# A depthwise convolution on TensorE: taps as pairs of 64x64 quarters, and gating between the granules of the projection

## The reference

```python
proj = u @ conv_w_in                                   # 256 x 1024 by 1024 x 1792
glu_in, mq = jnp.split(proj, [2 * CONV_DIM], axis=-1)  # CONV_DIM = 768
a, gate = jnp.split(glu_in + b_in, 2, axis=-1)
u = a * jax.nn.sigmoid(gate)
# causal, per channel, 31 taps: u[t] = sum_i dw[i] * u[t - 30 + i] + dw_b
u = depthwise_conv(u, dw) + dw_b
mix = jax.nn.silu(layer_norm(u, ln_g, ln_b))           # over the 768 channels
mem_out = memory_attention(mq, mk, mv, g_mq, g_mk)     # 4 heads of 64, 256 memory tokens
h = h + jnp.concatenate([mix, mem_out], axis=-1) @ w_out
```

## Time and profile before

| | us |
|---|---|
| three runs | 1823.68, 1824.05, 1825.80 |
| their median | 1824.05 |
| the profiled execution | 1827.86 |
| its span | 1826.1 |
| mean granted TensorE clock of its span | 0.984 of full |

### The profile page before, as it was taken

How to read it: one execution, slowest core, us unless ns; L and a number is a source line. 1 busy time by engine, 2 the same in 40 slices (tenths; PEclk the granted TensorE clock), 3 DMA queues, 4 the chain that set the end, 5 groups by cost and what they waited for, 6 DMA issues and landing times.

```text
span 1826.1 us, 22665 instructions
## 1 busy us (share of the span) xinstructions
PE 1756.5 (96%) x8300; PEld 1448.8 (79%) x8300; DVE 1346.3 (74%) x1211; ACT 1161.0 (64%) x1149; POOL 63.1 (3%) x64
## 2 busy tenths in 40 slices
PE   7899999989999998879999999999999999999998
PEld 6678888877788886668888888888888888888886
DVE  5664444675554457658888888888898888888888
ACT  5555553665444447547777777677777777776775
POOL 1110000230000010020000000000000000000000
PEclk9899999999999999889999999999999999999999
DMA  9554553644655561038989999999999999999995
GB/s 339 165 165 159 183 186 121 194 152 153 195 183 185 162 206 50 23 105 307 369 327 365 371 325 367 350 349 365 346 348 372 328 370 367 323 370 347 348 368 224
DMA packets 226406, 480.82 MB, mean 263 GB/s; under 512 B 11796, under 2 KB 48296, under 8 KB 226352
## 3 DMA queue, kind: packets, MB, share of 16 engines
q1 hardware_dynamic: 217056, 470.99, 72.6%
q10 hardware_dynamic: 9296, 9.11, 1.5%
HBM read 478.99 MB, written 2.65 MB: 264 GB/s over the span
## 4 chain that ended last, share of the span: by engine, by line
PE 53%; DVE 4%; ACT 3%; issue 2%; ACTq 0%; DVEq 0%; POOLq 0%; POOL 0%
PE bank L614 16%; PE bank L617 16%; PE bank L615 16%; PE bank L1125 2%; ACT w_hi L1661 1%; PE bank L1157 1%; PE bank L1038 1%; DVE x L2175 1%; DVE w_lo L2195 1%; ACT L1661 0%; DVE dwy L2076 0%; DVE stat L2076 0%; ACT y_hi L1649 0%; DVE w_lo L1718 0%; DVE rawmax L1815 0%
## 5 line engine op out<-in xcount | busy, mean ns | idle before, releaser
L2195 DVE TENSOR_TENSOR w_lo<-raw,w_hi 128x2048 fp32r<-128x2048 f32 x336 | 764.4, 2289 | 118.5 <-ACT w_hi L1661 115.5
L1661 ACT ACTIVATE w_hi<-raw 128x2048 fp32r<-128x2048 f32 x336 | 639.2, 1919 | 173.5 <-PE bank L617 173.4
L1718 DVE TENSOR_TENSOR w_lo<-raw,w_hi 128x2048 fp32r<-128x2048 f32 (+3 forms) x118 | 257.1, 2184 | 158.7 <-ACT w_hi L1227 158.4
L614 PE MATMUL bank<-w_hi,xg_hi 128*128 128x512 f32 x896 | 355.5, 397 | 5.8 <-DVE w_lo L2195 4.3
L617 PE MATMUL bank<-w_hi,xg_lo 128*128 128x512 f32 x896 | 350.4, 391 | 0.0
L615 PE MATMUL bank<-w_lo,xg_hi 128*128 128x512 f32 x896 | 349.9, 390 | 0.0
L1227 ACT ACTIVATE w_hi<-raw 128x2048 fp32r<-128x2048 f32 (+3 forms) x118 | 213.1, 1811 | 104.0 <-PE bank L617 93.2
L614 PE MATMUL bank<-w_hi,a_hi 128*128 128x512 f32 (+3 forms) x672 | 261.8, 390 | 14.1 <-DVE a_lo L2110 5.4
L615 PE MATMUL bank<-w_lo,a_hi 128*128 128x512 f32 (+3 forms) x672 | 255.5, 380 | 0.0
L617 PE MATMUL bank<-w_hi,a_lo 128*128 128x512 f32 (+3 forms) x672 | 255.3, 380 | 0.0
L614 PEld LDWEIGHTS bank<-w_hi,xg_hi 128*128 128x128 f32 x896 | 168.9, 189 | 42.4 <-DVE w_lo L2195 7.3
(11 more groups left out here) (226 smaller groups left out, 1695.4 us busy)
## 6 DMA issues: line engine op xcount, KB each, us to landing
raw<-in_moe_w_gate SPq DMA_DIRECT2D x114, 1024.0 KB, 6.8
raw<-in_moe_w_up SPq DMA_DIRECT2D x113, 1024.0 KB, 7.0
raw<-in_moe_w_down SPq DMA_DIRECT2D x112, 1024.0 KB, 6.3
raw<-in_w_mlp SPq DMA_DIRECT2D x32, 1024.0 KB, 5.2
raw<-in_ffn_w_gate SPq DMA_DIRECT2D x22, 512.0 KB, 3.8
raw<-in_ffn_w_up SPq DMA_DIRECT2D x22, 512.0 KB, 4.8
raw<-in_ffn_w_down SPq DMA_DIRECT2D x11, 1024.0 KB, 4.9
raw<-in_w_in SPq DMA_DIRECT2D x10, 1024.0 KB, 12.2
```

The costliest lines, as they stand in the source:

```text
L614: pe.matmul(o, hi, h, start=start, stop=False)
L1661: act.activation(w_hi[:, g % NSPLIT, :], raw_at(g, GRAN), ACT.Copy).then_inc(hi_made, 1)
L1718: dve.tensor_tensor(w_lo[:, g % NSPLIT, 0:n], raw_at(g, n), w_hi[:, g % NSPLIT, 0:n].bitcast(F32), ALU.subtract).then_inc(lo_made, 1)
L2195: dve.tensor_tensor(w_lo[:, g % NSPLIT, :], raw_at(g, GRAN), w_hi[:, g % NSPLIT, :].bitcast(F32), ALU.subtract).then_inc(lo_made, 1)
```

## The change

- **The projection.** The jobs become: value and gate columns of channel tiles 0 and 1 (512 columns, 256 of each, by two DMAs a granule), `mq` (256 columns), value and gate of tiles 2 and 3, value and gate of tiles 4 and 5. So a pair of tiles can be transposed and gated (`glu_t`, `gates`, `gated`) as soon as its own job is done. Transposes, scores, softmax and values of the memory attention are put between the granules, as in the other two blocks.
- **The taps.** TensorE takes 20 of the 31 taps, two at a time. A tap pair is four float32 matmuls of 64 rows by 64 columns, one for each quarter of the array: tap 2i on channels 0-63 (rows 0-63, columns 0-63) and on channels 64-127 (rows and columns 64-127), and tap 2i+1 on the two other quarters, which read `glu_x`, a copy of `glu` with its two halves of partitions exchanged. `glu_x` is made by DMAs inside SBUF (`crossed`, two of 64 x 2 x 256 for each pair of tiles), issued by ScalarE. The upper and the lower 64 rows write different banks, and VectorE adds both banks (`add_taps`). ScalarE writes two diagonals of 128 x 64 for a pair (`dw` and `dw_x`, a copy of the weights with exchanged halves), in a ring of 12 pairs. Each quarter counts its own semaphore `tap_used[n]`.
- **VectorE** takes 11 taps a tile, two tiles by turns, so that the second sum in `stat` falls away.
- **`out2`** begins with the memory attention's tiles: these are multiplied before the mean is known and while the squares are made. The rounded halves of the normalized tiles are made one tile at a time.

The core of the diff; the parts left out are the same edits on names, and the helpers `gates`, `gated`, `out_in2`, which wrap the loops of before:

```diff
-PE_TAPS = 16
-N_DIAG = 12
+PE_TAPS = 20
+TAP_PAIRS = PE_TAPS // 2
+DIAG_PAIRS = 12
+TAP_BANK = (2, 4, 0, 2, 0, 4)
...
-    stage("glu", t="adadad")
-    stage("qk2", t="aa")
-    stage("pv2", t="bb")
+    stage("mk2", t="a")
+    stage("glu0", t="ad")
+    stage("mq2", t="a")
+    stage("glu1", t="ad")
+    stage("pvm2a", t="b")
+    stage("pvm2b", t="b")
+    stage("glu2", t="ad")
...
-    CONV_JOBS = [(0, 512), (512, 512), (1024, 512), (1536, 256)]
+    CONV_JOBS = [(0, 512), (1536, 256), (512, 512), (1024, 512)]
...
+        if n == 256:
+            project(conv_in, c0, n)
+            continue
+        for half in range(2):
+            stream.append(([(rows(conv_in, half * 512, 4, u * CONV_TILES * P + c0 // 2, 256), None, u) for u in range(2)], 4, 512))
...
+        glu_x = sb("glu_x", [P, CONV_TILES, S + DW_K - 1], stack=layer)
...
-        diag = dwq[:].rearrange("p k s -> p (k s)").rearrange("p (n c) -> p n c", c=P)
-        stat = sb("stat", [P, 3, S], stack=layer)
+        diag = dwq[:].rearrange("p k s -> p (k s)").rearrange("p (n c) -> p n c", c=HD)
...
+            def mq2_t(kk):
+                if kk == 2:
+                    copied(j2 + 1)
+                    cols_t(at["mq2"]["t"], proj2, [MQ2, MQ2 + P])
+            def taps(k):
+                pe.wait_ge(glu_x_in[k // 2], 32)
+                ba, bb = bank[TAP_BANK[k]], bank[TAP_BANK[k] + 1]
+                for i in range(TAP_PAIRS):
+                    m = k * TAP_PAIRS + i
+                    pe.wait_ge(diag_made, 2 * m + 2)
+                    for n, (w, u, r, c, b) in enumerate(((0, glu, 0, 0, ba), (0, glu, HD, HD, bb),
+                                                         (1, glu_x, 0, HD, ba), (1, glu_x, HD, 0, bb))):
+                        tap = 2 * i + w
+                        mm = pe.matmul(b[c:c + HD, 0:S], diag[r:r + HD, 2 * (m % DIAG_PAIRS) + w, :], u[r:r + HD, k, tap:tap + S],
+                                       start=i == 0, stop=i == TAP_PAIRS - 1)
+                        mm.then_inc(tap_used[n], 1)
...
+            in2(0)
+            in2(1)
             pe.wait_ge(qk_made, 5)
-            t = at["qk2"]["t"]
-            cols_t(t, proj2, [MQ2, MQ2 + P])
-            cols_t(t + 1, kvm2, [0, P])
-            pe.wait_ge(t_act, act_steps(t + 1))
-            def taps(k):
-                if k >= 2:
-                    pe.wait_ge(dw_acc, k - 1)
-                for i in range(PE_TAPS):
-                    pe.wait_ge(diag_made, k * PE_TAPS + i + 1)
-                    mm = pe.matmul(bank[k % 2][:, 0:S], diag[:, (k * PE_TAPS + i) % N_DIAG, :], glu[:, k, i:i + S],
-                                   start=i == 0, stop=i == PE_TAPS - 1)
-                    mm.then_inc(tap_used, 1)
-                means = {4: (0, 1, 2), 5: (3,)}.get(k, ())
-                if k == 4:
-                    pe.wait_ge(s_exp, 4 * len(PAIRS))
-                for done in means:
-                    channel_mean(done)
-            def channel_mean(k):
-                return pe.matmul(bank[2][:, 0:S], onesm[:], dwy[:, k, :], start=k == 0, stop=k == CONV_TILES - 1)
-            pe.wait_ge(t_dve, dve_steps(at["glu"]["t"] + 5))
+            cols_t(at["mk2"]["t"], kvm2, [0, P])
+            in2(2)
+            glu_t(0)
+            in2(3)
+            in2(4, mq2_t)
+            pe.wait_ge(t_act, act_steps(at["mq2"]["t"]))
             scores(MEM2)
-            taps(0)
+            in2(5)
             scores(MEM2 + 1)
             probs_t(MEM2)
-            taps(1)
+            in2(6, lambda kk: glu_t(1) if kk == 2 else None)
             values(MEM2)
             probs_t(MEM2 + 1)
+            in2(7)
+            values(MEM2 + 1)
+            glu_t(2)
+            pe.wait_ge(s_exp, 4 * len(PAIRS))
+            taps(0)
+            pe.wait_ge(p_sb, 2 * len(PAIRS))
+            taps(1)
             taps(2)
-            values(MEM2 + 1)
-            for k in range(3, CONV_TILES):
-                taps(k)
-            pe.wait_ge(dw_acc, CONV_TILES)
+            pe.wait_ge(dw_acc, 1)
+            taps(3)
+            pe.wait_ge(t_dve, dve_steps(at["glu2"]["t"] + 1))
+            pe.wait_ge(t_dve, dve_steps(at["pvm2b"]["t"]))
+            channel_mean(0)
+            channel_mean(1)
+            channel_mean(2)
+            taps(4)
+            channel_mean(3)
+            taps(5)
...
+            out2_part(0, 0, (0,))
             for k in range(4, CONV_TILES):
                 mm = channel_mean(k)
             mm.then_inc(mu_psum, 1)
+            out2_part(0, 0, (1,))
+            out2_part(1, 0, (0, 1))
             for k in range(CONV_TILES):
                 pe.wait_ge(sqc_made, k + 1)
-                mm = pe.matmul(bank[3][:, 0:S], onesm[:], dwq[:, k, :], start=k == 0, stop=k == CONV_TILES - 1)
+                mm = pe.matmul(bank[7][:, 0:S], onesm[:], dwq[:, k, :], start=k == 0, stop=k == CONV_TILES - 1)
             mm.then_inc(var_psum, 1)
-            def fill_out2(i, kk):
-                if i == 0 and kk % 2 == 0:
-                    pe.wait_ge(ln_lo, kk // 2 + 1)
-                if i == 0 and kk == 0:
-                    pe.wait_ge(dw_acc, CONV_TILES)
-                    pe.wait_ge(cent_made, CONV_TILES)
-                    pe.wait_ge(sd_made, 1)
-                if i == 2 and kk == 0:
-                    pe.wait_ge(ln_lo, 3)
-                if i == 2 and kk == 2:
-                    pe.wait_ge(t_dve, dve_steps(PAIRS[MEM2 + 1].t))
-            out_jobs("out2", "mix2", "nffn1", fill_out2)
+            out2_part(0, 0, (2, 3))
+            out2_part(1, 0, (2, 3))
+            out2_part(0, 1, range(4))
+            out2_part(1, 1, range(4))
...
+            def crossed(p):
+                act.wait_ge(t_dve, dve_steps(at[f"glu{p}"]["t"] + 1))
+                for r in (0, HD):
+                    act.dma_start(glu_x[r:r + HD, 2 * p:2 * p + 2, DW_K - 1:], glu[HD - r:P - r, 2 * p:2 * p + 2, DW_K - 1:])\
+                        .then_inc(glu_x_in[p], 16)
+            def diagonals(first, last):
+                for m in range(first, last):
+                    k, i = divmod(m, TAP_PAIRS)
+                    if m >= DIAG_PAIRS and (m % 2 == 0 or m == first):
+                        for n in range(4):
+                            act.wait_ge(tap_used[n], m - m % 2 - DIAG_PAIRS + 2)
...
+                    for w, taps in enumerate((dw, dw_x)):
+                        act.activation(diag[:, 2 * (m % DIAG_PAIRS) + w, :], ident2[:], ACT.Copy,
+                                       scale=taps[:, k, 2 * i + w:2 * i + w + 1]).then_inc(diag_made, 1)
+            act.wait_ge(kv_act, 2)
+            act.wait_ge(kv_dve, 2)
+            square_heads(kvm2, 0, MEM_HEADS, None)
+            for r in (0, HD):
+                ins = act.activation(ident2[r:r + HD, :], ident[r:r + HD, r:r + HD], ACT.Copy)
+            chained(ins)
+            hi_to(g + 3)
...
+            gates(0)
+            hi_to(g + 5)
+            crossed(0)
+            out_in2(1)
+            square_heads(proj2, MQ2, MEM_HEADS, j + 1)
+            hi_to(g + 6)
+            t_copy(at["mq2"]["t"], memq[:], GMQ1)
             exps(MEM2)
-            diagonals(1)
+            hi_to(g + 7)
+            out_in2(2)
             probs_copy(MEM2)
             exps(MEM2 + 1)
+            hi_to(g + 8)
+            gates(1)
             mixed_hi(MEM2)
-            diagonals(2)
             probs_copy(MEM2 + 1)
-            diagonals(3)
+            crossed(1)
+            hi_to(g + 9)
+            diagonals(0, 6)
+            out_in2(3)
             mixed_hi(MEM2 + 1)
-            diagonals(4)
-            hi_to(at["out2"]["g"] + 2)
-            diagonals(CONV_TILES - 1)
+            gates(2)
+            diagonals(6, 12)
+            crossed(2)
+            diagonals(12, 20)
+            hi_to(g + 10)
+            diagonals(20, CONV_TILES * TAP_PAIRS)
...
+                act.wait_ge(silu2, k + 1)
+                act.activation(a_at(a_hi, "mix2", 2 + k)[:, 0, :], dwq[:, k, :], ACT.Copy).then_inc(ln_hi, 1)
...
+            def other_taps(p, first, last):
+                for i in range(PE_TAPS + first, PE_TAPS + last):
+                    for k in (2 * p, 2 * p + 1):
+                        u, y = glu[:, k, i:i + S], dwy[:, k, :]
+                        if i == PE_TAPS:
+                            ins = dve.tensor_scalar(y, u, dw[:, k, i:i + 1], dwb[:, k:k + 1], ALU.mult, ALU.add)
+                        else:
+                            dve.wait_ge(dve_own, own[0] - 1)
+                            ins = dve.scalar_tensor_tensor(y, u, dw[:, k, i:i + 1], y, ALU.mult, ALU.add)
+                        own[0] += 1
+                        ins.then_inc(dve_own, 1)
...
+                y = dwy[:, k, :]
+                chained(dve.tensor_tensor(y, y, bank[TAP_BANK[k]][:, 0:S], ALU.add))
+                dve.tensor_tensor(y, y, bank[TAP_BANK[k] + 1][:, 0:S], ALU.add).then_inc(dw_acc, 1)
...
+            sum_heads(N2MK)
+            chained(dve.memset(glu[:, :, 0:DW_K - 1], 0.0))
```

(87 more changed lines are left out.)

136 lines of the change are left out of this document (44 added, 92 removed).

## The result

The changed kernel takes 1807.76 us (median of five runs, 1806.51 to 1813.17). The kernel before takes 1825.80 us in five runs beside it. The ratio is 0.9901, 95% interval [0.9888, 0.9914]: 18 us, 1%, faster. The profiled execution took 1807.76 us, its span 1806.0, its mean granted clock 0.985.

A forecast was written before the change was run, and what follows sets the result against it. TensorE, busy 96%, was taken as the bound; the router's earlier start counts. Router 793.2 to 774.5 gives 18.7 us, less 1.3 handovers and 1.7 clock: 15.7, so 1824.05 becomes 1808.4 us, range 1803 to 1815 (chance 0.75).

The forecast's parts named there:

- The four quarters: TensorE's taps: four quarter matmuls run at once, so a tap pair costs 0.43 us, 0.45 with its semaphores.
- two at once: Rival for TensorE's taps: only two quarters overlap, a pair costs 0.88 us, time 1830; chance 0.11.
- one at a time: Rival for TensorE's taps: quarters run one after another, 1.77 us a pair, time 1883; chance 0.04.
- The projection (A): Start of in2 to first tap: in2 ends at 704.2, first tap at 707.6, before 701.8.
- keys' wait: In in2, ahead of the third granule: TensorE idles 4.8 us for the memory's keys, some 3.4 us at half speed.
- The taps (B): Tap stretch: ScalarE's diagonals set the pace, not TensorE; last tap at 740.5, before 756.2.
- the diagonal: ScalarE in the taps: a 64-wide diagonal takes near 0.27 us (0.24 to 0.293), 0.54 a pair.
- To the first normalized tile (C): Last tap to first a_lo, through means, squares and out2 pieces: 13.1 us, before 10.8.
- To the router (D): From first normalized tile to router: router and gain loads delay w_hi and w_lo; router at 774.5, before 793.2.
- Charges: Ahead of the router, taken off the 18.7 us gain: 1.3 for some 25 handovers and 1.7 for the clock.
- The rule on posts: Tap matmuls: each semaphore post adds 26.3 ns, making a pair 0.56 us and the time 2.2 us higher, 1810.6.
- Swallowed: Rival for the experts' loop: if bound by its loads, part of the lead is lost there, 1824; chance 0.02.

The follow-up runs named there:

- e8: Changed kernel with ScalarE writing one 128x64 diagonal per tap pair instead of two, read by all four quarters: 1809.1 us, ratio 0.9905.
- e3: Changed kernel with one semaphore post per tap pair, by the last of its four matmuls, instead of four: 1809.1 us, ratio 0.9890.
- best: Changed kernel with small loads behind the keys' square, squares summed before out2's memory tiles of granule two, w_hi and w_lo before the router/gain wait: 1798.9 us, ratio 0.9843.
- e2: Changed kernel with tap matmuls queued two pairs at a time, both matmuls of one quarter directly behind each other: 1811.8 us, ratio 0.9907.
- e4b: Changed kernel with ScalarE's seven small loads issued behind the memory keys' square and the fourth granule's w_hi: 1804.9 us, ratio 0.9879.
- e7: Changed kernel with the two memory tiles of out2's second granule behind the sum of the squares instead of ahead: 1805.2 us, ratio 0.9882.

## Why the prediction was right

- **The four quarters.** Right. Taken from rows that showed two at once only the earlier trace rows; a pair is 0.43, against 0.43 and 0.45 with its semaphores, which add nothing. The rival "two at once" is refuted by the eight records in 0.43 us, "one at a time" too.
- **The projection (A).** Right in place and size: keys' wait 4.75 (predicted 4.8), with 3.4 us at half the clock behind it. The first tap, in the clock of before, came at 708.9 (707.42 + 1.46), predicted 707.6; the charge for the clock, 1.7 us outside this sum, fell due here. There is luck in the 4.75: the issues took 4.2 us and not 7 x 0.42 = 2.9, and yet the keys were only 0.1 us later than laid out (666.6), so another step had been placed over 1 us too late.
- **The taps (B).** Right in half. ScalarE sets the pace in two tiles of six only; in the others it is TensorE. The term that was too high is the diagonal: 0.24, not 0.27, at the low end of its bounds. I had taken the saving by width from a square of 256 columns, which has no weight per partition, beside a diagonal, which has one; between diagonals of 128 and of 64 columns it is 0.054. The stretch was 30.3 us and not 32.9: 2.6 us, the largest miss. By e8, ScalarE's hold on the 30.3 is only 1.7.
- **To the first normalized tile (C).** The last tap to `out2`'s first tile is 13.6 us (737.76 to 751.38), predicted 13.1.
- **To the router (D).** `w_lo` of the fourth granule gates it, behind the gain's DMA, as predicted; router at 774.3 in the clock of before, predicted 774.5 without the charges.
- **Charges.** Of the 3.0 us taken off for handovers and clock, 2.4 came (1.3 + 0.5 + 0.6, by which A, C and D were longer than laid out). So the gain ahead of the router is 18.7 - 2.4 + 2.6 = 18.9, forecast 15.7. The median, 1807.76, met 1808.4 more closely than that by luck: the kernel before, run again, had a median 1.75 us above the one that I had set out from, and this hid most of the gain that I had missed.
- **The rule on posts.** Weighed at 2.2 us; e3 shows nothing of it.
- **"Swallowed".** Refuted: router to end is 1033.2 us (1806.0 - 772.83), before 1032.9, and it is no different in `best` (1032.7).

What was not in the prediction: that the order of work alone, in the two forms tried, gains nothing with the old split of the taps. I had thought of the lead as the taps' alone and gave the order no price of its own; asked by the experiment, I gave it 7 us, and that was wrong for both.

## What to carry to other kernels

Work that uses a quarter of the array could be packed four to a slot here, in float32 too, as long as something else makes the small operands at the same pace: price that engine first. A series of small DMA issues in front of an instruction that another engine's whole queue waits for cost about its full length (4.2 us of issues, 4.4 us of wait); put them behind it. Filler work belongs where TensorE waits, behind the short chain that ends the wait, not ahead of it. Moved there, 2.75 us of it gave 4.3, since the clock stayed up too.

## What the runs showed of the hardware that was not expected

- The order in which matmuls to the four quarters stand in the queue hardly mattered: 31.1 us in place of 30.3 for 60 pairs, with two in a row for each quarter. They start out of that order (e2).
- Four posts in 0.43 us cost nothing that shows (e3).
- On ScalarE 128 x 64 diagonals start 0.24 us apart, 128 x 128 ones 0.293: halving the width saves a fifth.
- In the changed kernel the granted clock was 0.50 for 3.4 us behind the wait of 4.75, and 0.79 and 0.52 in the two 5 us windows around the end of the wait of 4.45. The waits of 0.39 and 1.7 us in the same places (e4b, e7) left it at 1.00. It fell behind shorter waits too: 2.7 us in the kernel before.
- The same program's start of `in2` lies between 648.1 and 655.4 us over the traces, ahead of any edit. In comparing single traces only intervals behind a common mark tell an effect of a few us, and these too differ, by 0.7 us ahead of the taps and by 1.6 behind them.
